# Prompt attention's reciprocal sums: one full float product per group, or two split-float products

## The reference, cut to what matters

```python
def attend_selected(q, k_sel, v_sel, valid):
    bsz, t, h, d = q.shape
    qg = q.reshape(bsz, t, N_KV_HEADS, h // N_KV_HEADS, d)
    s = jnp.einsum('btgrd,btkgd->btgrk', qg, k_sel).astype(jnp.float32) * (d ** -0.5)
    s = jnp.where(valid[:, :, None, None, :], s, -jnp.inf)
    p = jax.nn.softmax(s, axis=-1).astype(v_sel.dtype)
    o = jnp.einsum('btgrk,btkgd->btgrd', p, v_sel)
    return o.reshape(bsz, t, h * d)
```

## Time and profile before

| | |
|---|---|
| median of 3 runs | 1977.17 us (1976.7 to 1978.89) |
| span of the profiled execution | 1973.8 us; its own time is not given apart from the three runs (1977.17, 1978.89, 1976.7) |
| mean granted TensorE clock | 0.975 of full speed |
| busy share of the span | PE 94%, DVE 44%, ACT 40%, POOL 33% |
| prompt attention | from about 1442 to 1636 us after the span's start |

### The profile page before, as it was taken

The page is one execution under the profiler, slowest core; times in us unless marked ns, Lnnn a source line. Parts: engine busy times, 40 slices in busy tenths (PEclk is TensorE's granted clock), DMA queues, the critical chain, the costliest instruction groups (busy, mean ns, idle before and its releaser), DMA issues. The chain is left out here.

```text
span 1973.8 us, 30722 instructions
## 1 busy us (share of the span) xinstructions
PE 1863.0 (94%) x11000; PEld 1647.2 (83%) x11000; DVE 862.2 (44%) x1653; ACT 793.2 (40%) x1148; POOL 649.9 (33%) x397
## 2 busy tenths in 40 slices
PE   7999999899999999999979989999989998699998
PEld 7999999899887888779969549999966765499997
DVE  4113333311114444033254877687778634512433
ACT  4233333212243333233235675567865554402211
POOL 4333323265333334654522131111132002354220
PEclk9999999999999999999989899999999999899999
DMA  6223222222222222331123110312231006531111
GB/s 187 75 65 85 74 74 74 64 77 83 85 85 85 85 85 86 95 109 33 32 64 122 31 56 22 89 43 66 88 121 31 1 1 209 186 99 43 44 55 45
DMA packets 226179, 150.76 MB, mean 76 GB/s; under 512 B 16754, under 2 KB 219250, under 8 KB 225714
## 3 DMA queue, kind: packets, MB, share of 16 engines
q1 hardware_dynamic: 210754, 125.78, 21.6%
q0 software_dynamic: 5152, 14.48, 2.4%
q10 hardware_dynamic: 10192, 9.46, 1.4%
HBM read 133.24 MB, written 16.43 MB: 76 GB/s over the span
## 5 line engine op out<-in xcount | busy, mean ns | idle before, releaser
L434 POOL TENSOR_TENSOR wlo<-wraw,whi 128x1024 fp32r<-128x1024 f32 x177 | 430.2, 2431 | 722.4 <-ACT whi L429 720.3
L446 PE MATMUL PS<-hhi_g,whi 128*128 128x288 f32 (+1 forms) x1152 | 324.0, 335 | 12.2 <-POOL wlo L434 7.2
L429 ACT ACTIVATE whi<-wraw 128x1024 fp32r<-128x1024 f32 x177 | 186.6, 1055 | 343.0 <-PE PS L446 324.6
L446 PE MATMUL PS<-hhi_g,wlo 128*128 128x288 f32 (+1 forms) x1152 | 317.1, 330 | 0.0
L446 PE MATMUL PS<-hlo_g,whi 128*128 128x288 f32 (+1 forms) x1152 | 316.9, 329 | 0.0
L446 PE MATMUL PS<-hhi,whi 128*128 128x364 f32 x1176 | 269.7, 338 | 12.8 <-DVE hlo L559 6.8
L446 PE MATMUL PS<-hlo,whi 128*128 128x364 f32 x1176 | 262.0, 331 | 0.0
L446 PE MATMUL PS<-hhi,wlo 128*128 128x364 f32 x1176 | 260.6, 330 | 0.0
L446 PEld LDWEIGHTS PS<-hhi_g,whi 128*128 128x128 f32 x1152 | 195.7, 189 | 31.1 <-issue 6.6
L446 PEld LDWEIGHTS PS<-hhi,whi 128*128 128x128 f32 x1176 | 204.0, 191 | 20.4 <-issue 13.9
L446 PEld LDWEIGHTS PS<-hhi_g,wlo 128*128 128x128 f32 x1152 | 196.4, 189 | 17.7
(11 more groups left out here) (392 smaller groups left out, 2726.4 us busy)
## 6 DMA issues: line engine op xcount, KB each, us to landing
wraw<-in_w_in_a_dram SPq DMA_DIRECT2D x96, 512.0 KB, 3.9
wraw<-in_w_out_a_dram SPq DMA_DIRECT2D x32, 512.0 KB, 4.0
wraw<-in_w_in_b_dram SPq DMA_DIRECT2D x25, 512.0 KB, 3.7
wraw<-in_w_pe_gate_dram SPq DMA_DIRECT2D x16, 512.0 KB, 4.2
kpg<-in_cache_k_dram SPq DMA_DIRECT2D x64, 128.0 KB, 2.8
vpg<-in_cache_v_dram POOLq DMA_DIRECT2D x64, 128.0 KB, 2.4
xs<-xT SPq DMA_DIRECT2D x1, 4368.0 KB, 12.6
xT<-xs SPq DMA_DIRECT2D x1, 4368.0 KB, 14.0
```

Of the source, the lines that this page charges most:

```text
L429: nc.scalar.activation(whi[par][:], wraw[par][:], ACT.Copy).then_inc(w_hi, 1)
L434: nc.gpsimd.tensor_tensor(wlo[par][:], wraw[par][:], whi[par][:].bitcast(F32), ALU.subtract).then_inc(w_lo, 1)
L446: mm = nc.tensor.matmul(o, w[par][:, k, :], r(k, c0, cn), start=first and i == 0 and n == 0, stop=last and i == KD - 1 and n == 2)
```

## The change

The group's reciprocals are split as the weights are: `arhi` is `ars` rounded to float32r, `arlo` the rest. GpSimd makes both (a copy, then a subtraction, each waited for by its own next instruction), then two diagonal blocks, `rdhi` and `rdlo`, both of type float32r. TensorE multiplies float32r ones by the one and then by the other into the same bank. The ones are copied once, ahead of the loop. `rdhi`, the ones and the small tiles lie in the last 4 KB per partition of the region of `xT`, which is free then; `rdlo` takes the place of `rdiag`, and the samples' `new_logits` takes that place later, as before.

```diff
+        pl = region(D0 - 2 * BANK * 4, D0)
+        rdhi = pl("rdhi", [P, REP, P], F32R)
+        onesr = pl("onesr", [P, P], F32R)
+        arhi, arlo = pl("arhi", [P, REP], F32R), pl("arlo", [P, REP])
...
-        rdiag = pl("rdiag", [P, REP, P])
+        rdlo = pl("rdlo", [P, REP, P], F32R)
...
             pool.wait_ge(w_used, U_O)
+            own.link(nc.gpsimd.tensor_copy(onesr[:], ones[:]))
             for i in range(NBLK * NKV):
                 pool.wait_ge(at_["rs"], i + 1)
                 if i:
                     pool.wait_ge(at_["tr"], SPREAD_AT[i - 1] + 1)
-                nc.gpsimd.tensor_tensor(rdiag[:], ident[:].unsqueeze(1).broadcast_to((P, REP, P)),
-                                        ars[:, REP * i:REP * i + REP].unsqueeze(2).broadcast_to((P, REP, P)),
-                                        ALU.mult).then_inc(at_["dg"], 1)
+                part = ars[:, REP * i:REP * i + REP]
+                own.link(nc.gpsimd.tensor_copy(arhi[:], part))
+                own.link(nc.gpsimd.tensor_tensor(arlo[:], part, arhi[:].bitcast(F32), ALU.subtract))
+                for half, diag in ((arhi[:].bitcast(F32), rdhi), (arlo[:], rdlo)):
+                    nc.gpsimd.tensor_tensor(diag[:], ident[:].unsqueeze(1).broadcast_to((P, REP, P)),
+                                            half.unsqueeze(2).broadcast_to((P, REP, P)), ALU.mult).then_inc(at_["dg"], 1)
...
             def spread_sums(i):
 
                 j = SPREAD_AT[i]
-                pe.wait_ge(at_["dg"], i + 1)
+                pe.wait_ge(at_["dg"], 2 * i + 2)
                 pe.wait_ge(at_["pt"], j - 1)
-                nc.tensor.matmul(PS[:, 4 + j % 2, :], ones[:], rdiag[:].rearrange("p r q -> p (r q)"), start=True,
+                nc.tensor.matmul(PS[:, 4 + j % 2, :], onesr[:], rdhi[:].rearrange("p r q -> p (r q)"), start=True,
+                                 stop=False)
+                nc.tensor.matmul(PS[:, 4 + j % 2, :], onesr[:], rdlo[:].rearrange("p r q -> p (r q)"), start=False,
                                  stop=True).then_inc(at_["tr"], 1)
```

More of the change, by code:

```diff
@@ L269, in hybrid_trunk @@
         kpg.append(nc.alloc_sbuf_tensor_at("kpg2", [P, NPAGE, NKV * DH], F32, offset=X0))
-        rdiag = pl("rdiag", [P, REP, P])
+        rdlo = pl("rdlo", [P, REP, P], F32R)
+        RDLO = D0 + (NBLK * REP * P + 2 * NPAGE * NKV * DH) * 4
         pl = region(H2, END)
@@ L286, in hybrid_trunk @@
         heads, fold, new_max = rsb[:, 0], rsb[:, 1, 0:NS], rsb[0:NS, 1, NS:NS + DEC_B]
-        new_logits = rdiag[0:NS].rearrange("p r q -> p (r q)")
+        new_logits = nc.alloc_sbuf_tensor_at("new_logits", [NS, BANK], F32, offset=RDLO)[:]
         def old_probs(b):
```

## The result

The changed kernel takes 1983.69 us (median of 8 runs, 1982.94 to 1985.73), the kernel before 1977.96 us in 8 runs of the same comparison (1974.71 to 1980.3). The ratio is 1.0031, interval 1.0021 to 1.0041: slower by 0.3%, some 6 us. I had forecast no change (1977.6).

The account below looks back on a forecast made before the run. TensorE was taken to bound the late blocks, with early groups waiting on GpSimd's diagonal. +4.30 early and -3.89 late gave +0.4 us on the 1973.8 span, 1974.2; with 3.4 to the median, 1977.6 us, range 1973.9 to 1981.2.

Parts of the forecast that it names:

- the sum over the groups: All 16 groups: +4.30 us for the early ones, -3.89 for group 5 and the nine late ones, together +0.4.
- group 1 (taken at 0): Early group 1: its +1.06 us falls into TensorE's later idle 1.26 us waiting for VectorE, so 0.
- groups 3 to 6: Early groups: 3 and 4 together +1.12 us, group 5 gains 0.40, group 6 costs 1.06.
- group 8 (taken at -0.29): Tightest late group: gains 0.40 us less 0.11, the 1.46 us chain against 1.35 of time in hand.
- What bounds the kernel: Prompt attention: TensorE's queue paces late blocks; in first blocks three engines hand work round, the diagonal last in four groups.
- GpSimd's chain: GpSimd per group: second diagonal 1.04 us plus 0.42 for copy, subtraction and hand-overs; TensorE told 1.46 us later.
- rival B: Early groups' longer TensorE waits: clock falls once more (1979.3, chance 0.4) or twice (1981.0; two or more 0.08).
- rival C: Seven early groups: GpSimd's longer work holds VectorE's multiply for `anb`, 3.6 us, 1981.2; chance 0.09 in all.
- 1.40 in hand: Group 8: time from the diagonal's end, 1523.71, to its spread's start, 1525.11, in the kernel before.
- None from group 7 on: Trace sign: TensorE waits for diagonals in groups 0 to 4 and 6, about 7 us more, none from group 7.
- The late groups: Group 5 and groups 7 to 15: gain 0.40 us each, less 0.11 in group 8, -3.89 in all.
- Rival D: TensorE: float32r products cost 0.43 us each, so nothing is won; 6.3 us of waits, 1983.6; chance 0.02.

Follow-up runs that it names:

- the delay alone: Kernel before, with three memsets on GpSimd between the diagonal and its signal to TensorE; 1986.46 us, ratio 1.0034.
- filled waits: Changed kernel, with unread float32r products of ones put ahead of TensorE's waits in groups 1 to 4, 6 and 8; 1981.02 us, ratio 1.0017 to the kernel before.
- GpSimd's part alone: Changed kernel's four GpSimd operations, the last writing the full float diagonal, with TensorE's full product as before; 1989.32 us, ratio 1.0063 to the kernel before.
- the hold alone: Kernel before, with a second GpSimd diagonal into a spare tile after the signal to TensorE; 1976.85 us, ratio 0.9985.
- small operations on VectorE: Changed kernel, with the 128x4 copy and subtraction moved from GpSimd to VectorE behind the reciprocal; 1980.76 us, ratio 1.0011 to the kernel before.
- split products shifted: Changed kernel, with each spread and the multiply of the heads' outputs one step later in the queues; 1970.26 us, ratio 0.9961 to the kernel before.
- the late split without group 8: Kernel before, with split products only in groups 7 and 9 to 15; 1973.07 us, ratio 0.9974.
- the late split: Kernel before, with split products only in groups 7 to 15; 1975.4 us, ratio 0.9986.

## Why the prediction was wrong, step by step

The step that failed is the sum over the groups. It had +4.30 us for the early groups and -3.89 for the late ones, each diagonal costing GpSimd 1.04 us wherever it falls, each wait standing alone, and the clock and VectorE kept out as rivals. Measured, the stage is 7.8 us longer. The terms that were wrong are group 1 (taken at 0), groups 3 to 6, and above all group 8 (taken at -0.29).

*What bounds the kernel.* Right: late blocks by TensorE, early groups by the diagonal. Right too that a float32r pair wins 0.40: from group 9 to group 15 the change gains 2.39 us, 0.40 for each of six steps.

*GpSimd's chain.* The sum of 1.46 was near: two small operations 0.19 and 0.20 with 0.08 behind each, and 1.00 from diagonal to diagonal, make 1.55. The copy at 0.1 was under-sized; its row of comparison, a memset, was an operation of another kind. In the groups that wait, TensorE is held 0.96 us by the full product and 0.56 by the split ones, not 0.87 and 0.47, so their difference of 0.40 stands.

The starts of the spreads that my terms give, beside those measured, in us later than before:

| spread of group | 0 | 1 | 2 | 3 | 4 | 5 | 6 | 7 | 8 | 9 | 15 |
|---|---|---|---|---|---|---|---|---|---|---|---|
| by the terms of the sum | 1.46 | 2.52 | 2.52 | 3.10 | 3.64 | 3.24 | 4.30 | 3.90 | 3.61 | 3.21 | 0.81 |
| measured | 1.54 | 2.67 | 3.68 | 4.34 | 5.34 | 5.16 | 7.37 | 6.89 | 9.24 | 10.40 | 8.01 |
| more | 0.08 | 0.15 | 1.16 | 1.24 | 1.70 | 1.92 | 3.07 | 2.99 | 5.63 | 7.19 | 7.20 |

*Group 1, taken at 0, was wrong in this kernel: 1.0 us.* I had set TensorE's later idle time of 1.26 against the delay. With the delay alone that is what happens: there the lateness only grows from 3.17 at group 1 to 3.47 at group 2 (spreads at 10.09 and 19.18), although group 2 adds 1.75 of its own (3.37 us from reciprocal to spread, where it was 1.62), so 1.45 was swallowed. In the change two things undo it. VectorE, which ends that wait, is itself late, since its copies into `qb` are held by the diagonals, 1.49 us where they had taken 0.91:

```profile
1461.33 1.49 DVE L1848 COPY qb<-qT 128x64 f32<-128x64 f32 x8
...
1463.76 0.70 PE L2387 MATMUL PS<-kT,qT 128*128 128x256 f32 x2 [0.70 <-DVE amx L1821]
```

and the clock falls near 1465, which was rival B. In the kernel with filled waits, which has not this fall, 0.8 is swallowed (lateness 3.79 and 4.23, with 1.73 added by group 2's own chain and 0.50 won between, a spread behind the fillers holding TensorE only 0.46 us). In the change it is 0.3 by the same count.

*Groups 3 to 6: 1.9 us.* In group 4 the copy is held (0.62 us) and the low diagonal too (1.29), 0.7 together, where the one diagonal before had been held by 0.4 (1.45); with the chain's own 0.1 that makes 0.4 of the 0.5 that is added there. From group 5 to group 6, 1.15 is added, and 1.06 of it lies ahead of the reciprocal of group 6, which comes 5.82 us late, where group 5's spread (5.16) less the gain of 0.40 gives 4.76. Between the reciprocals of these two groups VectorE has no idle time in either kernel, so it and not TensorE sets the time. The stretch takes 13.87 us where it took 13.10, and one multiply in it is held beside the second diagonal:

```profile
1496.28 0.93 DVE L1825 TENSOR_TENSOR anb<-amx,nqs 128x1 f32<-128x1 f32 x1
```

It takes 0.93 us in place of 0.16, and that is the whole 0.77. With GpSimd's part alone the stretch takes 13.87 us as well, although no product is shorter there, so the gain of 0.40 does not come out at this place; with the delay alone it takes 13.43 and with the hold alone 13.33, where the same multiply takes 0.39. Here, then, rival C was at work as I had described it, for 0.8 us.

*Group 8, taken at -0.29, failed by most: 2.6 us, and 1.6 behind it.* Its own spread is 2.35 us later than the one before, and the next, with the fall of the clock between them, another 1.16. I had checked the 1.40 in hand against the chain's length alone, and bounded a hold by group 6's 0.5 us. The second diagonal starts later than the one diagonal did before, and there VectorE runs a scan of 2.41 us. "None from group 7 on" was wrong for that reason. With memsets in that place the wait is gone (0.09 us), and so it is where the low diagonal comes ahead of the scan (0.19).

*The late groups.* Right: the surplus stays at 7.2 from group 9 to the end. The clock is part of it. Behind group 6 a fall stood in the kernel before as well; of the two that are new, the one behind group 8 costs 1.6 us, and the one behind group 1 some 0.6, by the run with filled waits.

*The rivals.* Two more falls (B) and GpSimd and VectorE in each other's way (C) came together; I had priced them apart and given slower 0.15 in all. That the falls were two more and not one is in part luck, since the same wait of 2.07 us was followed by one in two executions and by none in a third. In C the direction was mostly wrong: but for the 0.8 us above, what counts is not VectorE held in `anb` but GpSimd held in what TensorE waits for. Rival D's number, 1983.6, is the time measured by chance alone: it had the late groups gain nothing, and they gain 0.40 each.

## What to carry to other kernels

Before a helper engine's chain is lengthened, compare the time in hand with the new chain at each place where it is waited for, and look at what the engine that can hold it (here VectorE) runs in the *new* position of each operation, not in the old one. An exchange of matmul time for helper time pays where the helper has a step's lead: here moving the waiting product one step later in the queue turned a loss of 0.3% into a gain of 0.4%, where the same move gave the full product 0.1%. Idle times that lie near one that already made the clock fall should be priced with the fall, and together, since one delay feeds the next.

## What the runs showed of the hardware

- A 128x4 copy on GpSimd takes 0.19 us and a subtraction 0.20, with 0.08 us from the end to the next instruction that waits for it; a 128x1 memset took 0.098.
- Two GpSimd diagonals of 1.04 us that do not wait for each other start 1.00 us apart.
- A GpSimd operation that reads SBUF, started 0.02 us after VectorE's scan of 2.41 us, took 3.23 us in place of 1.04. Memsets were not held beside the same scan. Four memsets of other groups took 0.16 to 0.22 us longer than their like, each beside a `tensor_scalar` of VectorE.
- With the small operations on VectorE, and with the split products shifted, the low diagonal of group 8 started 0.04 to 0.05 us ahead of VectorE's multiply for `anb`. There the diagonal took 1.03 to 1.04 us and the multiply 1.01 in place of 0.16.
- A full float product of 512 columns held TensorE 0.96 us after a wait and 0.87 without one; two float32r products in its place held it 0.56 after a wait.
- The same wait of 2.07 us before the spread of group 6 was followed by a fall of the granted clock in two executions (the kernel before, and the late split without group 8), and not in a third (the late split).
- Filling TensorE's waits with products that nobody reads made the kernel 2.7 us faster by keeping the clock up (one fall in prompt attention in place of three).
